# A hybrid attention layer: the v projection fed feature by feature from a transposed copy of x

## The chip, the cores and the metric

One core of a Trainium2 chip. The metric is the device time of one execution in microseconds; lower is better. All data are float32; products are made accurate by splitting each operand into a high part (a reduced-precision float, "fp32r") and a low part (the rest), and by summing three matmul passes: high x high, low x high, high x low.

## The reference

```python
h = rmsnorm(x, pre_g)                      # x: 1024 tokens x 1024 features
p = einsum('btd,de->bte', h, w_in)         # 3328 columns
aq, ak, av, ag, bq, bk, bv, bg = split_projection(p)
ya = sliding_window_sink_attention(aq, ak, av, sinks) * silu(ag)
yb = differential_attention(bq, bk, bv, lam, ...) * silu(bg)
y = einsum('bte,ed->btd', concat(ya, yb), w_out)
return x + rmsnorm(y, post_g)

def rmsnorm(x, g):
    return x * rsqrt(mean(x * x, axis=-1) + 1e-6) * g
```

The norm's factor is one number per token, the gain g one number per feature. v is the 512 columns bv and the 128 columns av.

## The kernel before

The program is written engine by engine, and the engines meet at counting semaphores. It has two stages and an ending.

*The v stage.* v_sb holds tokens on the partitions. The 640 columns are taken as two halves of 320 (`VG`), the 1024 tokens as 8 tiles of 128. One group is one tile and one half: 8 feature slabs x 3 passes = 24 matmuls into one of the two banks of `proj`, then an eviction by ScalarE (`store_v`). Group n is tile n % 8 of half n // 8. To feed it, a tile of x is loaded with tokens on the partitions (`load_x`, three buffers), squared and summed (`square_x`, ScalarE), its factor is made by GpSimd (`root`), it is normalised by VectorE (`norm_x`, L909, against the gain row that TensorE has spread over the partitions into `pre_g`, L1185), turned by eight transposes into `scores` (`turn_x`, L1160), and split into hT_hi (`high_h`, ScalarE, L726) and hT_lo (`low_h`, VectorE, L917). The weights of v are split by ScalarE (`high_wv`), VectorE and GpSimd (both `low_wv`). The tiles go one after another: tile t+1 is turned while tile t is projected.

*The units.* 21 units of 128 columns of w_in (`UNITS`) are projected with the weights stationary and all tokens moving, each in two halves of 512 tokens and six pieces of four matmuls (L1250), into the two banks of `proj`. A schedule written out at build time (`SCHEDULE`) weaves these pieces between the steps of the attention blocks. Unit n needs `w_raw` loaded by SP (`load_w`), w_hi by ScalarE (`high_weights`, L746), w_lo by GpSimd (`low_weights`, L652). SP's queue is in order: the loads for units 0 and 1 are issued during the v stage; ahead of the load for unit 2 stand the two copies of v into `v_shift`, which wait for all 16 evictions:

```python
sp.wait_ge(pads_made, 1)
sp.wait_ge(v_stored, 2 * TILES)
...
for n in range(2, NU):
    load_w(n)
```

VectorE makes the constants of the attention (distances, slopes, lambda: `constants`, L931 to L954) behind its last split of the v stage.

*The ending* projects the output tile by tile (`out_project`, L1354), normalises it and adds x.

Of the kernel before, what the change touches and what calls it, by code (L numbers as in the profile page):

```python
# [75 lines left out]
XS = 3  # L76
WARM_UP = (2, 8)
WV_AT = 5
# [160 lines left out]
def hybrid_layer(nc, x, w_in, w_out, pre_norm_g, post_norm_g, sinks, lambda_q1, lambda_k1,  # L239
# [46 lines left out]
    wv_raw = place("wv_raw", 120, [P, KT, V_WIDTH])  # L286
    x_in = place("x_in", 140, [P, XS, D_MODEL])
    wv_hi = place("wv_hi", 152, [P, KT, V_WIDTH], F32R)
    wv_lo = place("wv_lo", 172, [P, KT, V_WIDTH], F32R)
    g_rows = place("g_rows", 84, [P, D_MODEL])  # L290
    ones = place("ones", 116, [P, P])
    squares = place("squares", 201.75, [P, D_MODEL])
    lam_in = place("lam_in", 118, [P, 4, HEAD_DIM])

# [14 lines left out]
    x_square = column(TILES)  # L309
    x_mean = column(TILES)  # L310
    x_scale = column(TILES)
    min_b = column(2 * B_UNITS)
    sum_b = column(2 * B_UNITS)
    inv_b = column(2 * B_UNITS)
# [11 lines left out]
    neg_half = column(4)  # L326
# [20 lines left out]
    pre_g = banks  # L347
# [3 lines left out]

    x_loaded = [sem(f"x_loaded{i}") for i in range(XS)]
    wv_loaded = [sem(f"wv_loaded{i}") for i in range(6)]
    w_loaded = [sem(f"w_loaded{i}") for i in range(RAW)]
    wo_loaded = [sem(f"wo_loaded{i}") for i in range(WO_RAW)]
    g_row_loaded = sem("g_row_loaded")
    ones_made = sem("ones_made")
    g_zeroed = sem("g_zeroed")
    pre_g_spread = sem("pre_g_spread")
    wv_lo_early = sem("wv_lo_early")  # L360
# [13 lines left out]
    x_squared = sem("x_squared")  # L374
    x_meaned = sem("x_meaned")
    x_scaled = sem("x_scaled")
    x_normed = sem("x_normed")
    x_turned = sem("x_turned")
    h_hi_ready = sem("h_hi_ready")
    h_lo_ready = sem("h_lo_ready")  # L380
    wv_hi_ready = sem("wv_hi_ready")
    wv_lo_ready = sem("wv_lo_ready")
    v_projected = sem("v_projected")
# [44 lines left out]
    def x_turned_at(t):  # L428

        return scores[:, 1024 * (t % 2):1024 * (t % 2) + 1024].rearrange("p (k c) -> p k c", c=P)  # L430

# [25 lines left out]
    def feature_parts(t):  # L457


        return [slice(0, KT // 2), slice(KT // 2, KT)] if t < 2 else [slice(0, KT)]  # L460

    def tile_count(t, part=None):


        before = sum(len(feature_parts(m)) for m in range(t))
        return before + (len(feature_parts(t)) if part is None else part + 1)
# [43 lines left out]
    def wait_proj_free(engine, filling):  # L510

        before = filling - 2
        if before < 0:
            return
        if before < 2 * TILES:
            engine.wait_ge(v_stored, before + 1)
# [42 lines left out]
    v_runs = [[(BV, VG, 0)], [(BV + VG, B_WIDTH - VG, VG), (AV, P, B_WIDTH)]]  # L559

    with nc.Block() as block:

        @block.sync
        def _(sp):
            def load_x(t):
                if t >= XS:
                    sp.wait_ge(x_turned, tile_count(t - XS))
                sp.dma_start(x_in[:, t % XS, :], x[0, t * P:(t + 1) * P, :]).then_inc(x_loaded[t % XS], 16)

            sp.dma_start(g_rows[P - 1:P, :], pre_norm_g[0:1, :]).then_inc(g_row_loaded, 16)  # L570
            for t in range(3):
                if t:
                    load_x(t)
                if t == 2:
                    break
                for part in (2 * t, 2 * t + 1):
                    k = slice(2 * part, 2 * part + 2)
                    sp.dma_start(wv_raw[:, k, 0:VG], w_cols[:, k, BV:BV + VG]).then_inc(wv_loaded[part], 16)
            for i, (first, count, to) in enumerate(v_runs[1]):
                load_x(3 + i)  # L580
                sp.dma_start(wv_raw[:, :, to:to + count],
                             w_cols[:, :, first:first + count]).then_inc(wv_loaded[4 + i], 16)
# [34 lines left out]
            for t in range(5, TILES):  # L617
                load_x(t)
                if t < 7:
                    load_w(t - 5)  # L620
                if t == 5:
                    load_small()
# [24 lines left out]
        def _(pool):  # L647
# [16 lines left out]
            pool.wait_ge(half_made, 1)  # L664
            def low_wv(part):
                k, cols = slice(2 * part, 2 * part + 2), slice(0, VG)
                pool.wait_ge(wv_hi_ready, part + 1)
                nc.gpsimd.tensor_tensor(wv_lo[:, k, cols], wv_raw[:, k, cols], wv_hi[:, k, cols].bitcast(F32),
                                        ALU.subtract).then_inc(wv_lo_early, 1)

            for t in range(TILES):
                pool.wait_ge(x_squared, t + 1)
                nc.gpsimd.tensor_scalar(x_mean[:, t:t + 1], x_square[:, t:t + 1], 1.0, EPS, ALU.mult,
                                        ALU.add).then_inc(x_meaned, 1)
                pool.wait_ge(x_meaned, t + 1)
                root(x_scale[:, t:t + 1], x_mean[:, t:t + 1], 1, x_scaled)
                if t == 0:
                    low_wv(0)
                elif t == 1:
                    low_wv(1)  # L680
                    low_wv(2)
# [3 lines left out]
                           allow_small_or_imprecise_dtypes=True).then_inc(dist_made, 1)  # L685
            for n in (0, 1):
                for part in range(LOWS):
                    low_weights(n, part)
# [29 lines left out]
        def _(act):  # L718
            def high_wv(k, cols, ready):
                act.wait_ge(wv_loaded[ready], 16)  # L720
                nc.scalar.activation(wv_hi[:, k, cols], wv_raw[:, k, cols], ACT.Copy).then_inc(wv_hi_ready, 1)

            def high_h(t, part=0):
                k = feature_parts(t)[part]
                act.wait_ge(x_turned, tile_count(t, part))
                nc.scalar.activation(hT_hi[:, k, t * P:(t + 1) * P], x_turned_at(t)[:, k],  # L726
                                     ACT.Copy).then_inc(h_hi_ready, 1)

            def square_x(t):
                act.wait_ge(x_loaded[t % XS], 16 * (t // XS + 1))  # L730
                if t:
                    act.wait_ge(x_squared, t)
                nc.scalar.activation(squares[:, :], x_in[:, t % XS, :], ACT.Square, scale=D_MODEL ** -0.5,
                                     accum_out=x_square[:, t:t + 1]).then_inc(x_squared, 1)

            def store_v(t, g):
                n = TILES * g + t
                act.wait_ge(v_projected, n + 1)
# [637 lines left out]
```

## Time and profile before

| | us |
|---|---|
| median of 3 runs | 526.04 |
| lowest to highest | 525.56 to 527.71 |
| profiled execution, its own time | 523.85 |
| its span, first to last instruction | 522.0 |
| TensorE busy | 507.3 |
| VectorE busy | 263.9 |
| ScalarE busy | 250.6 |
| GpSimd busy | 115.1 |

The engines are PE (TensorE; PEld are its weight loads), DVE (VectorE), ACT (ScalarE), POOL (GpSimd) and SP. L12 is line 12 of the kernel. A matmul's duration reaches from its start to the end of its pipeline, so durations of neighbours overlap; their pace is the distance of their starts. A plain f32 matmul is two instructions in the profile, one in fp32r a single one.

### The profile page before, as it was taken

What the parts mean: (1) busy time and instruction counts of PE and PEld (TensorE: products, weight loads), DVE (VectorE), ACT (ScalarE), POOL (GpSimd) and SP (SyncE); (2) the same over time, 40 slices, a digit from 0 to 9 for tenths busy, and PEclk for the clock granted to TensorE, in tenths of its full rate; (3) what the DMA queues carried; (4) which work ended last, traced back from release to release, by engine and by line L of the source; (5) the groups of instructions that cost most, each with busy time, mean ns of one, the idle gap of its engine ahead of it and who ended that gap; (6) DMA issues with size and microseconds to landing.
All of it is one profiled execution on the core that took longest, in us unless ns stands there. A gap on an engine that the chain in (4) does not pass through costs nothing.

```text
span 522.0 us, 7538 instructions
## 1 busy us (share of the span) xinstructions
PE 507.3 (97%) x2766; PEld 423.4 (81%) x2766; DVE 263.9 (51%) x648; ACT 250.6 (48%) x615; POOL 115.1 (22%) x157
## 2 busy tenths in 40 slices
PE   7999999999999999999999989999999999999995
PEld 4999997888878787888886767778788888888884
DVE  5655002565565546444547768544654375433332
ACT  5654213556476566556478667533645372322211
POOL 4221204030222120323044243322302260000000
PEclk9999999999999999999999999999999999999998
DMA  8630024130101110110101110111000754332222
GB/s 291 203 123 1 1 46 123 32 80 1 40 15 27 42 41 0 41 40 2 41 1 41 41 42 1 41 41 41 1 1 0 162 162 125 109 130 81 82 84 77
DMA packets 41190, 32.05 MB, mean 61 GB/s; under 512 B 18561, under 2 KB 35905, under 8 KB 41154
## 3 DMA queue, kind: packets, MB, share of 16 engines
q1 hardware_dynamic: 38706, 26.85, 18.4%
q10 hardware_dynamic: 2448, 4.72, 2.4%
q8 instruction: 22, 0.36, 0.3%
q14 instruction: 14, 0.11, 0.1%
HBM read 26.88 MB, written 4.19 MB: 60 GB/s over the span
## 4 chain that ended last, share of the span: by engine, by line
PE 87%; ACT 4%; issue 3%; DVE 3%; DMA 1%; POOL 1%; SPq 0%; DVEq 0%; POOLq 0%; ACTq 0%
PE proj L1250 40%; PE scores L1354 15%; PE proj L1172 11%; PE scores L1269 6%; PE banks L1290 5%; PE banks L1280 3%; PE banks L1335 2%; PE scores L1315 1%; PE banks L1323 1%; PE scores L1160 1%; DMA w_raw<-in_w_in 1%; ACT weights L822 1%; ACT k_stack L802 1%; PE banks L1185 1%; ACT w_hi L746 1%
## 5 line engine op out<-in xcount | busy, mean ns | idle before, releaser
L652 POOL TENSOR_TENSOR w_lo<-w_raw,w_hi 128x256 fp32r<-128x256 f32 x84 | 61.0, 756 | 183.4 <-ACT w_hi L746 183.4
L1250 PE MATMUL proj<-hT_hi,w_hi 128*128 128x512 f32 x336 | 89.9, 400 | 1.1 <-DVE k_stack L1009 0.6
L1250 PE MATMUL proj<-hT_hi,w_lo 128*128 128x512 f32 x336 | 89.4, 400 | 0.0
L1250 PE MATMUL proj<-hT_lo,w_hi 128*128 128x512 f32 x336 | 88.5, 399 | 0.0
L1064 DVE CUSTOM_DVE_ANT_0 weights<-scores,dist_b 128x128 f32<-128x128 f32 (+7 forms) x64 | 45.9, 754 | 53.8 <-PE scores L1269 53.6
L1250 PEld LDWEIGHTS proj<-hT_hi,w_hi 128*128 128x128 f32 x336 | 60.5, 188 | 14.3 <-DVE k_stack L1009 1.0
L1250 PEld LDWEIGHTS proj<-hT_hi,w_lo 128*128 128x128 f32 x336 | 60.6, 188 | 13.3 <-issue 1.9
L1250 PEld LDWEIGHTS proj<-hT_lo,w_hi 128*128 128x128 f32 x336 | 60.6, 188 | 11.8 <-issue 0.8
L822 ACT ACTIVATE weights<-weights,small 128x128 f32<-128x128 f32 (+7 forms) x64 | 49.0, 767 | 15.2 <-DVE small L1064 15.2
L832 ACT ACTIVATE weightsT<-banks 128x512 f32<-128x512 f32 (+3 forms) x48 | 23.6, 491 | 56.0 <-PE banks L1280 55.9
L1269 PE MATMUL scores<-k_stack,q_stack 128*128 128x512 f32 (+3 forms) x192 | 41.8, 353 | 0.0
L1290 PEld LDWEIGHTS banks<-v_sb,weightsT 128*128 128x128 f32 x288 | 36.2, 191 | 4.5 <-ACT weightsT L832 2.1
L1290 PE MATMUL banks<-v_sb,weightsT 128*128 128x128 f32 x288 | 37.8, 276 | 0.1
L656 POOL TENSOR_TENSOR small<-small 128x1 f32<-128x1 f32 (+1 forms) x24 | 17.2, 718 | 85.4 <-DVE small L1137 84.1
L1269 PEld LDWEIGHTS scores<-k_stack,q_stack 128*128 128x128 f32 x192 | 31.9, 189 | 4.9 <-DVE k_stack L1009 0.4
L891 ACT ACTIVATE banks<-scores 128x512 f32<-128x512 f32 x16 | 9.3, 582 | 53.3 <-PE scores L1354 53.3
L1095 DVE CUSTOM_DVE_ANT_0 a_weights<-scores,dist_a,small 128x128 f32<-128x128 f32 x64 | 22.5, 406 | 18.3 <-PE scores L1315 18.3
L1048 DVE SCALAR_TENSOR_TENSOR weights<-weights,small,weights 128x512 f32<-128x512 f32 (+3 forms) x48 | 31.1, 676 | 1.1
L1354 PE MATMUL scores<-wo_hi,hT_hi 128*128 128x512 f32 x128 | 31.6, 389 | 0.0
L1354 PE MATMUL scores<-wo_lo,hT_hi 128*128 128x512 f32 x128 | 31.6, 389 | 0.0
L1354 PE MATMUL scores<-wo_hi,hT_lo 128*128 128x512 f32 x128 | 31.6, 389 | 0.0
L1009 DVE TENSOR_TENSOR k_stack<-proj,k_stack 64x512 fp32r<-64x512 f32 x32 | 22.0, 688 | 12.7 <-ACT k_stack L802 11.9
(114 smaller groups left out, 721.9 us busy)
## 6 DMA issues: line engine op xcount, KB each, us to landing
w_raw<-in_w_in SPq DMA_DIRECT2D x13, 512.0 KB, 3.8
w_raw<-in_w_in SPq DMA_DIRECT2D x16, 256.0 KB, 3.7
x_res<-in_x SPq DMA_DIRECT2D x8, 512.0 KB, 4.5
out<-y_out ACTq DMA_DIRECT2D x16, 256.0 KB, 2.3
x_in<-in_x SPq DMA_DIRECT2D x7, 512.0 KB, 6.0
wv_raw<-in_w_in SPq DMA_DIRECT2D x4, 320.0 KB, 6.0
wo_early<-in_w_out SPq DMA_DIRECT2D x4, 256.0 KB, 4.5
w_raw<-in_w_out SPq DMA_DIRECT2D x4, 256.0 KB, 6.6
```

The lines of the kernel that those rows point to most:

```text
L652: nc.gpsimd.tensor_tensor(w_lo[:, n % SPLIT, k], w_raw[:, n % RAW, k], w_hi[:, n % SPLIT, k].bitcast(F32), ALU.subtract).then_inc(w_lo_rea ...
L822: nc.scalar.activation(w, w, ACT.Exp, scale=-1.0, bias=min_b[:, 2 * u + m:2 * u + m + 1], accum_out=sum_b[:, 2 * u + m:2 * u + m + 1]).the ...
L832: nc.scalar.activation(weightsT[:, 4 * r:4 * r + blocks, :], turned[:, 0:P * blocks].rearrange("p (b q) -> p b q", q=P), ACT.Copy).then_in ...
L1009: nc.vector.tensor_tensor(k_lo[part, m, tokens], source[own, :], k_hi[own, m, tokens].bitcast(F32), ALU.subtract).then_inc(stack_lo, 1)
L1048: nc.vector.scalar_tensor_tensor(w0, w1, mix_b[:, u:u + 1], w0, ALU.mult, ALU.add).then_inc(b_mixed, 1)
L1064: nc.vector.tensor_tensor_reduce(out=weights_1[:, 0:keys] if m else weights_0[:, u % 2, 0:keys], in0=scores[:, 1024 * m:1024 * m + keys], ...
L1095: nc.vector.tensor_tensor_reduce(out=a_weights_of(c)[:, j, :], in0=scores[:, a_scores_at(c, j):a_scores_at(c, j) + P], in1=dist_a[:, min(c ...
L1172: done = nc.tensor.matmul(proj[:, n % 2, 0:VG], h[:, k, tokens], w[:, k, cols], start=(first and k == ks[0]), stop=(last and k == ks[-1]))
L1250: last = nc.tensor.matmul(to, w[:, slot, k, :], h[:, k, HALF * half:HALF * half + HALF], start=(p == 0 and k == first), stop=(p == PIECES ...
L1269: last = nc.tensor.matmul(scores[:, 1024 * m + first:1024 * m + first + width], q_stack[head][m][:, P * block_:P * block_ + P], k[:, m, fi ...
L1290: last = nc.tensor.matmul(mixed[:, P * (u % 4):P * (u % 4) + P], weightsT[:, b, :], v_sb[:, b, P * head:P * head + P], start=(b == 0), sto ...
L1354: last = nc.tensor.matmul(scores[:, at:at + HALF], y[:, k, tokens], w[:, k, cols], start=(p == 0 and k == 0), stop=(p == PASSES - 1 and k ...
```

## The change

The host hands over x a second time, transposed (`xT`, features first), and the gain as a column per slab (`g_columns`). The kernel no longer turns x.

- Slabs of 128 features are loaded: x_all[:, k, :] (all 1024 tokens) and the 320 columns of w_in for the first half of v, in turn, k = 0 to 7. All are issued on SP's queue with no wait; slab 0 of x comes in two halves from ScalarE's queue.
- v's operand is x times the gain, without the token's factor. hT_hi and hT_lo hold this first (`high_x`, `low_x`). The factor is applied per token (that is, per partition) at the eviction: `store_v` has a scale.
- Seven token tiles are summed side by side, one PSUM bank each, slab by slab (`K_MAJOR = 7`). The eighth tile and the whole second half of v follow group by group (24 matmuls each).
- The squares are summed over slabs elementwise (ScalarE squares, VectorE adds), then over the partitions by eight one-column matmuls (`x_sums`). GpSimd takes all 8 x 128 roots in one instruction.
- The normalised h is still needed for the units. The factors are put on diagonals, spread over all partitions by two f32 matmuls (`scale_rows`), x_all is normalised in place beside the second half of v, and hT_hi and hT_lo are written a second time (`high_again` and h_lo_again) tile by tile, each after the group that reads the old tile.
- The iotas of GpSimd move to its start; the constants move ahead of the normalisation on VectorE. The splits of the second half's weights are four pieces on ScalarE and GpSimd.

```diff
-            for t in range(TILES):
-                store_v(t, 0)
-                if t + 3 < TILES:
-                    square_x(t + 3)
-                if t + 2 < TILES:
-                    high_h(t + 2)
...
+            def high_x(k):
+                for part, tokens in enumerate(token_parts(k)):
+                    act.wait_ge(x_loaded[k + part if k == 0 else k + 1], 16)
+                    nc.scalar.activation(hT_hi[:, k, tokens], x_all[:, k, tokens], ACT.Copy,
+                                         scale=g_column[:, k:k + 1]).then_inc(h_hi_ready, 1)
+            def square_x(k):
+                if k >= 3:
+                    act.wait_ge(squares_added, k - 2)
+                to = squared[k % 2] if k else square_sum
+                nc.scalar.activation(to[:, :], x_all[:, k, :], ACT.Square).then_inc(x_squared, 1)
...
+                nc.scalar.activation(v_sb[:, t, VG * g:VG * (g + 1)], v_bank(n), ACT.Copy,
+                                     scale=x_scale[:, t:t + 1]).then_inc(v_stored, 1)
+            def high_again(t):
+                tokens = slice(P * t, P * t + P)
+                act.wait_ge(x_normed, KT)
+                act.wait_ge(v_projected, TILES + t + 1)
+                nc.scalar.activation(hT_hi[:, :, tokens], x_all[:, :, tokens], ACT.Copy).then_inc(h_hi_again, 1)
...
+            for k in range(KT):
+                high_x(k)
+                if k:
+                    act.wait_ge(wv_loaded[k], 16)
+                    nc.scalar.activation(wv_hi[:, 0, k], wv_raw[:, 0, k], ACT.Copy).then_inc(wv_hi_ready, 1)
+                square_x(k)
...
+            for k in range(1, KT):
+                low_x(k)
+                low_wv(k)
+                if k > 1:
+                    add_squares(k - 1)
+            add_squares(KT - 1)
+            dve.wait_ge(x_summed, 1)
+            nc.vector.tensor_scalar(x_mean, x_sums, 1.0 / D_MODEL, EPS, ALU.mult, ALU.add).then_inc(x_meaned, 1)
...
+            constants()
+            dve.wait_ge(scale_spread, 2)
+            for k in range(KT):
+                nc.vector.scalar_tensor_tensor(x_all[:, k, :], x_all[:, k, :], g_column[:, k:k + 1],
+                                               scale_rows[:, :], ALU.mult, ALU.mult).then_inc(x_normed, 1)
...
+            for _ in range(WARM_UP):
+                nc.tensor.matmul(turned[:, 0:P], ones[:, :], ones[:, :], start=True, stop=True)
+            for k in range(KT):
...
+                if k < KT - 1:
+                    for p, ready in enumerate((h_hi_ready, h_lo_ready)):
+                        for part, tokens in enumerate(token_parts(k)):
+                            pe.wait_ge(ready, part_count(k, part))
+                            for t in range(tokens.start // P, min(tokens.stop // P, K_MAJOR)):
+                                project_v(t, k, p)
+                    pe.wait_ge(wv_lo_ready, k + 1)
+                    for t in range(K_MAJOR):
+                        project_v(t, k, 2)
...
+            pe.wait_ge(squares_added, KT - 1)
             for t in range(TILES):
+                done = nc.tensor.matmul(x_sums[:, t:t + 1], square_sum[:, P * t:P * t + P], ones[:, 0:1],
+                                        start=True, stop=True)
+            done.then_inc(x_summed, 1)
+            for n in range(K_MAJOR, 2 * TILES):
+                if n >= TILES:
+                    wait_v_bank(pe, n)
+                if n == TILES + 1:
+                    pe.wait_ge(diagonals_made, TILES)
+                    pe.wait_ge(v_stored, TILES)
+                    for half in range(2):
+                        cols = slice(HALF * half, HALF * half + HALF)
+                        nc.tensor.matmul(scale_rows[:, cols], ones[:, :], diagonals[:, cols],
+                                         start=True, stop=True).then_inc(scale_spread, 1)
...
+                        if n == 0:
+                            pe.wait_ge(h_hi_again, TILES // 2 * (half + 1))
                     which, first = divmod(p * KP, KT)
+                    if n == 0 and which == 1:
+                        pe.wait_ge(h_lo_again, TILES // 2 * (half + 1))
```

`token_parts(k)` is two halves of 512 tokens for k = 0 and 1, all 1024 tokens for the others.

## Rows read from the trace of the kernel before

**Rows 1.** The page: busy time of the engines, and the span in 40 slices.

```profile
PE 507.3 (97%) x2766; PEld 423.4 (81%) x2766; DVE 263.9 (51%) x648; ACT 250.6 (48%) x615; POOL 115.1 (22%) x157
...
PEclk9999999999999999999999999999999999999998
```

**Rows 2.** The chain of waits: start, length, what, count.

```profile
38.48 0.87 PE scores L1160 x8
39.35 34.03 PE proj L1172 x232
73.94 0.73 SPq L627
75.43 5.59 DMA w_raw<-in_w_in
81.05 1.06 ACT w_hi L746
...
84.77 11.18 PE proj L1250 x48
...
154.59 1.87 PE banks L1290 x16
```

**Rows 3.** Timeline of TensorE, end of the v stage (wait in brackets).

```profile
72.04 1.34 PE L1172 MATMUL proj<-wv_lo,hT_hi 128*128 128x320 f32 x8
73.21 2.00 PE L1250 MATMUL proj<-hT_hi,w_hi 128*128 128x512 f32 x8
...
84.77 2.11 PE L1250 MATMUL proj<-hT_hi,w_hi 128*128 128x512 f32 x8 [0.49 <-DVE q_stack L1004]
```

**Rows 4.** Timeline of TensorE, the start.

```profile
1.69 0.69 PE L1179 MATMUL proj<-ident 128*128 128x128 f32 x2 [1.69 <-POOL ident L662]
3.19 3.75 PE L1185 MATMUL banks<-g_rows,ones 128*128 128x512 f32 x4 [0.81 <-DVE g_rows L965]
6.74 1.20 PE L1188 MATMUL proj<-ident 128*128 128x128 f32 x8
...
9.06 0.56 PE L1172 MATMUL proj<-wv_hi,hT_hi 128*128 128x320 f32 x2 [0.25 <-ACT hT_hi L726]
```

**Rows 5.** Windows of 1 us: busy by engine, granted clock, DMA share, GB/s.

```profile
1.00:2.00 1.00, 0.31 (x2) 0.29 (x2) 0.91 (x1) 0.86 (x1) 0.39 (x2) 1.00 0.36 82
2.00:3.00 1.00, 0.38 (x2) 0.00 (x0) 0.82 (x1) 0.42 (x1) 0.00 (x0) 1.00 0.91 348
3.00:4.00 1.00, 0.81 (x1) 0.50 (x2) 0.09 (x1) 0.02 (x1) 0.00 (x0) 1.00 0.92 299
4.00:5.00 1.00, 1.00 (x2) 0.34 (x1) 0.00 (x0) 1.00 (x2) 0.00 (x0) 1.00 0.91 288
```

**Rows 6.** Groups of instructions by shape, 0 to 75 us: busy, mean ns of one.

```profile
L909 DVE SCALAR_TENSOR_TENSOR x_in<-x_in,small,banks 128x1024 f32<-128x1024 f32 x6 | 7.7, 1282 | 9.3 <-POOL small L656 9.3
L733 ACT ACTIVATE squares<-x_in 128x1024 f32<-128x1024 f32 x7 | 7.4, 1055 | 1.9 <-DMA x_in<-in_x 1.9
...
L917 DVE TENSOR_TENSOR hT_lo<-scores,hT_hi 128x1024 fp32r<-128x1024 f32 x6 | 7.3, 1219 | 2.7 <-ACT hT_hi L726 2.7
L739 ACT ACTIVATE v_sb<-proj 128x320 f32<-128x320 f32 x16 | 7.0, 438 | 31.7 <-PE proj L1172 31.5
L726 ACT ACTIVATE hT_hi<-scores 128x1024 fp32r<-128x1024 f32 x6 | 6.2, 1029 | 4.5 <-PE scores L1160 4.4
...
L668 POOL TENSOR_TENSOR wv_lo<-wv_raw,wv_hi 128x640 fp32r<-128x640 f32 x3 | 4.6, 1557 | 0.0
L656 POOL TENSOR_TENSOR small<-small 128x1 f32<-128x1 f32 x8 | 4.4, 553 | 0.7
...
L721 ACT ACTIVATE wv_hi<-wv_raw 128x640 fp32r<-128x640 f32 x4 | 2.8, 732 | 0.0
...
L726 ACT ACTIVATE hT_hi<-scores 128x512 fp32r<-128x512 f32 x4 | 2.3, 595 | 3.7 <-PE scores L1160 3.7
...
L922 DVE TENSOR_TENSOR wv_lo<-wv_raw,wv_hi 128x640 fp32r<-128x640 f32 x1 | 0.8, 817 | 0.0
```

**Rows 7.** Timeline of VectorE, first and last of the constants.

```profile
44.63 0.22 DVE L931 CUSTOM_DVE_ANT_0 junk<-lam_in 128x64 f32<-128x64 f32 x1
...
48.64 0.11 DVE L954 MEMSET dist_a<- 128x64 f32 x1
```

More of the change, by code:

```diff
@@ L284, in hybrid_layer @@
     small = place("small", 206.25, [P, 392])
[L286 to L292, printed above, removed]
+    x_all = place("x_all", 120, [P, KT, SEQ])
+    wv_hi = place("wv_hi", 152, [P, 2, KT, VG], F32R)
+    wv_lo = place("wv_lo", 172, [P, 2, KT, VG], F32R)
+    wv_raw = place("wv_raw", 72, [P, 2, KT, VG])
+    squared = [place("squared0", 92, [P, SEQ]), place("squared1", 192, [P, SEQ])]
+    diagonals = place("diagonals", 92, [P, SEQ])
+    square_sum = place("square_sum", 201.75, [P, SEQ])
     lam_in = place("lam_in", 118, [P, 4, HEAD_DIM])
+    ones = place("ones", 119.5, [P, P])
     wo_hi = place("wo_hi", 96, [P, KT, D_MODEL], F32R)
@@ L615, in load_wo @@
                     to += count
[L617 to L622, printed above, removed]
+            load_w(0)
+            load_small()
+            load_w(1)
             sp.wait_ge(pads_made, 1)
@@ L685, in _ @@
                            allow_small_or_imprecise_dtypes=True).then_inc(dist_made, 1)
+            pool.wait_ge(half_made, 1)
+            for part in range(KT // 2):
+                if part == 2:
+                    pool.wait_ge(x_meaned, 1)
+                    root(x_scale, x_mean, TILES, x_scaled)
+                k = slice(2 * part, 2 * part + 2)
+                pool.wait_ge(wv_hi_late, part + 1)
+                nc.gpsimd.tensor_tensor(wv_lo[:, 1, k], wv_raw[:, 1, k], wv_hi[:, 1, k].bitcast(F32),
+                                        ALU.subtract).then_inc(wv_lo_late, 1)
             for n in (0, 1):
@@ L718, in _ @@
         def _(act):
[L719 to L727, printed above, removed]
@@ L962, in make_lambda @@
                 nc.vector.tensor_scalar(neg_lam, lam_dif, LAMBDA_INIT, None, ALU.subtract).then_inc(consts_made, 1)
-            for part in (slice(0, 96), slice(96, P - 1)):
-                nc.vector.memset(g_rows[part, :], 0.0).then_inc(g_zeroed, 1)
-            norm_x(0)
-            dve.wait_ge(x_loaded[1], 16)
-            dve.wait_ge(x_squared, 1)
-            nc.vector.tensor_tensor_reduce(out=squares[:, :], in0=x_in[:, 1, :], in1=x_in[:, 1, :],
-                                           scale=1.0 / D_MODEL, scalar=0.0, op0=ALU.mult, op1=ALU.add,
-                                           accum_out=x_square[:, 1:2]).then_inc(x_squared, 1)
@@ L1164, in _, with project_v @@
             V_PASSES = ((hT_hi, wv_hi), (hT_lo, wv_hi), (hT_hi, wv_lo))
-            def project_v(t, g, p, ks, first=False, last=False):
-                n = TILES * g + t
+            def project_v(n, k, p):
+                g, t = divmod(n, TILES)
                 h, w = V_PASSES[p]
-                tokens, cols = slice(P * t, P * t + P), slice(VG * g, VG * (g + 1))
-                for k in ks:
-                    done = nc.tensor.matmul(proj[:, n % 2, 0:VG], h[:, k, tokens], w[:, k, cols],
-                                            start=(first and k == ks[0]), stop=(last and k == ks[-1]))
-                if last:
-                    done.then_inc(v_projected, 1)
@@ L1177, in _ @@
-            pe.wait_ge(ident_made, 2)
-            for _ in range(WARM_UP[0]):
-                nc.tensor.transpose(proj[:, 1, 0:P], ident[:, :], ident[:, :])
-            pe.wait_ge(ones_made, 1)
-            pe.wait_ge(g_zeroed, 2)
-            pe.wait_ge(g_row_loaded, 16)
-            for half in range(2):
-                cols = slice(HALF * half, HALF * half + HALF)
-                nc.tensor.matmul(pre_g[:, cols], ones[:, :], g_rows[:, cols],
-                                 start=True, stop=True).then_inc(pre_g_spread, 1)
@@ L1228, in _ @@
-            pe.wait_ge(wv_hi_ready, 6)
-            for t in range(TILES):
-                wait_proj_free(pe, TILES + t)
-                project_v(t, 1, 0, ALL, first=True)
-                project_v(t, 1, 1, ALL)
-                if t == 0:
-                    pe.wait_ge(wv_lo_ready, 3)
-                project_v(t, 1, 2, ALL, last=True)
+                return nc.tensor.matmul(v_bank(n), h[:, k, P * t:P * t + P], w[:, g, k, :],
+                                        start=(k == 0 and p == 0), stop=(k == KT - 1 and p == PASSES - 1))
```

300 lines of the change are left out of this document (129 added, 171 removed).

## The prediction

> **What bounds the kernel now.** I read the page first: TensorE is busy 97% of the span at a granted clock of 9 tenths in every slice but the last, so time is won by taking work off TensorE or by closing an idle stretch of it [rows 1]. Then the chain of waits: from the fourth transposed tile on it is TensorE alone, eight transposes in 0.87 us and 24 matmuls of the v projection between them, until 232 matmuls in a row end in 34.03 us, 0.1467 us each [rows 2]. So one group of 24 matmuls (one token tile, one half of v) costs 3.52 us, and the 16 groups 56.3 us. The 64 transposes (8 tiles of 0.87 us) cost 6.96 us more. The first matmul of the projection units starts at 73.21 us [rows 3]. 73.21 - 56.3 - 6.96 leaves 9.9 us: that is what the start costs, in pauses and in slow instructions.
>
> The timeline of TensorE shows what is in these 9.9 us [rows 4]. It waits for the identity until 1.69, spreads the gain row from 3.19 (held by the zeroing of 127 rows on VectorE), runs eight idle transposes, and has its first v matmul at 9.06. The four instructions of the spread run from 3.19 to 6.74, 0.89 us each; they are f32 with 512 columns. f32 instructions with 128 columns take 1.87 us for 16, 0.117 each, in the middle of the kernel [rows 2], so 512 columns should take four times that, 0.47. They took about twice as long: though the granted clock of those microseconds reads 1.00, the high level of 2.4 GHz [rows 5], these instructions ran as at the lower one, 1.2 GHz. TensorE had done nothing but two transposes before.
>
> **What goes.** (a) The 64 transposes: -6.96 us. (b) The chain ahead of the first matmul, x to square to root to normalise to transpose to h_hi, ends at 9.06. Of the 9.9 us, 9.06 less the 0.87 of the first tile's transposes lie ahead of that matmul, and 1.7 us are pauses behind it (h_hi and h_lo of the first two tiles); both go. The squares, the normalisation and the splits that leave VectorE and ScalarE were beside TensorE later than that and give nothing by themselves.
>
> **What comes at the start.** Features first, the first matmul needs the gain column, the first half slab of x, and slab 0 of the weights. By the windows of DMA, 82 + 348 + 299 = 729 KB had moved by 4.0 us and 1,017 KB by 5.0 [rows 5]. Slab 0 is 512 KB of x plus 160 KB of weights, 688 thousand bytes; half of x is there at about 3.3 and the weights slab at about 3.6. ScalarE splits the half (0.60 us for 512 columns [rows 6]) until about 4.0, VectorE copies the weights meanwhile. The warm-up is now eight f32 matmuls of 128 columns, 16 instructions. At the lower clock one takes twice 0.107 to 0.117; from about 1.1 us they last until about 4.7. So v starts near 4.7 us (bounds: 4.2 if the clock rises early, 6.0 if slab 0 is there only with the 1,017 KB of 5.0 us and a split follows). If TensorE's instructions keep the low pace until 6.74 as in [rows 4], slab 0 loses up to 1.1 us; I take 0.4, as it is now continuously busy from 1.1 and not from 3.19.
>
> **The slab stage, who paces it.** Per slab TensorE has 7 tiles x 3 passes = 21 matmuls x 0.1467 = 3.08 us. VectorE: h_lo of 1024 columns with a scale 1.28 us (the scalar-tensor-tensor row), wv_lo of 320 columns about 0.49 (a line through 0.82 at 640 and 1.22 at 1024), the sum of squares 1.22: 2.99 us. ScalarE: h_hi 1.03, wv_hi about 0.46 (0.73 at 640, less 320 columns at the 0.84 ns that lie between 0.60 at 512 and 1.03 at 1024), square 1.05: 2.5 us [rows 6]. DMA: 688 KB at 288 to 348 GB/s is 2.0 to 2.4 us [rows 5]. TensorE is the slowest by 0.09 over VectorE, and busy times overlap a little with the next start, so it paces the stage. But ScalarE's square k waits for the addition of k-2, so ScalarE and VectorE are locked together; walking the two orders by hand, h_lo of slab 3 is ready at 13.8 and of slab 7 at 25.8, wv_lo of slab 7 at 26.3, where TensorE comes at 4.7 + 7 x 3.08 = 26.3. I allow 0.4 us of small waits (bounds 0 and 2.0, the latter if VectorE's period is 3.3). Eight slabs: 8 x 3.08 = 24.6.
>
> **What is added on TensorE.** x_sums: 8 f32 matmuls of one column, 16 instructions. Each loads 128 weight columns; the nearest row is 0.117 us per f32 instruction, 1.9 us in all, with one column in place of 128. I take 1.4 (bounds 0.9 and 3.4, at half speed). The sums of squares are ready at about 28.7, before the slabs end at 29.7-30: no wait. scale_rows: two f32 matmuls of 512 columns, 4 instructions at 0.47: 1.9 us at the full rate; 3.6 if they went as in [rows 4]. I take 1.8.
>
> **Covers of the rest.** After the sums come group 7 (3.52 us), then group 8, which needs one v bank emptied. The chain in between is mean on VectorE, root on GpSimd (0.55 us), one eviction (0.44): about 1.6 us with hand-overs, cover 3.52. GpSimd must first do two of the late wv_lo parts (1.56 us each [rows 6]), from about 26.8 to 29.9, before the mean is there; parts 3 and 4 end near 35, needed near 36.8. Group 9 needs only the eight diagonals (ready near 34); the constants, 44.63 to 48.75 before, 4.1 us [rows 7], go from about 34 to 38 while group 8 runs, and the spread ends near 39.7. If this cover were gone, h would be late by what is missing, not v. The normalisation is 8 x 1.28 = 10.3 us on VectorE, to about 50; ScalarE then makes h_hi again for tile m once group 8+m has been read, in the order of the evictions: tiles 0-3 by about 58, tile 7 at 64.9 + 0.25 + 0.44 + 1.03 = 66.6, and h_lo of it at 67.9. Unit 0, first half, wants tiles 0-3 at about 65 (cover 7 us); its second half wants tile 7 at 65 + 5.6 = 70.6 (24 matmuls, 0.233 each by the 48 of the chain [rows 2]; cover 3.9). So the second pass of splits costs nothing.
>
> On the SP queue everything of v is issued with no wait, then w_raw 0, the six small loads, w_raw 1; 6.8 MB for v at 300 GB/s are in by 23 us, the small ones by 30. The load for unit 2 still stands behind the wait for all 16 evictions: issue 73.94, landed 81.05, and its split [rows 2]. That chain is tied to the end of v and not to the clock on the wall, so it moves with it; TensorE's 0.49 us pause at 84.77 stays [rows 3]. Behind it the schedule is unchanged.
>
> **Sum.** 4.7 + 0.4 (clock) + 24.6 + 0.4 (waits) + 1.4 + 7.04 (groups 7, 8) + 1.8 + 24.64 (groups 9 to 15) = 65.0 us, against 73.21: -8.2 us. The profiled execution has 522.0 of span and 523.85 of its own time, the runs a median of 526.04; the difference of 2.2 us is outside what I change, so I take the 8.2 off the median: 517.8.
>
> **Rivals.**
> - *Forecast, TensorE paces the slabs* (0.75): 515.5 to 520.
> - *The suppliers pace them* (0.12). For it: VectorE's 2.99 is only 3% under 3.08, and the lock with ScalarE adds hand-overs. Against: TensorE's own share of work is the only one that can't shrink. At 3.3 to 3.6 us a slab it costs 8 x 0.2 to 0.5 = 1.8 to 4.2 us: 519.5 to 522.
> - *The clock falls in the slab loop* (0.04), the one on the other side. The loop over features spends 3.08 us of TensorE's work per load of data; with pauses between slabs TensorE may run as in [rows 4]. A stretch at half speed costs half its length; the gain of 8.2 is eaten after 16.4 us of it, 5 of the 8 slabs; all 8 slabs give 24.6 more, 542. Against it: the old kernel also had 1.7 us of pauses behind 9.06, and its granted clock stayed at the high level [rows 1]. The Trainium skill ("TensorE: Matmul & The Clock Gate", section on HAM oscillation) describes just this loop, one feature tile per load with a wait of some microseconds, as the one that falls to the low clock at every tile. By that rule the time would be up to 542; by the supply worked out above the waits are tenths of a microsecond, and it would not apply.
> - *h is late at unit 0* (0.04): the second pass of splits stands behind evictions and the normalisation. Each microsecond beyond the 3.9 of cover costs one; 8 us late gives 522.
> - *Nothing comes through* (0.02): the 8 us reappear before a load; 526. Against: no wait of SP is later than its evictions.
> - *Better* (0.03): start at 4.2, cheap sums, no waits: 515.0.
>
> **Range and chances.** The bounds add up to -1.8 and, in the usual mix, +3.5 around 517.8, with half a microsecond between medians: 515.2 to 521.3. A measurement tells 0.5%, 2.6 us, from nothing. Faster by that (under 523.4): the forecast, the better case, the suppliers, most of late h: 0.92. Same 0.04 (nothing comes through, part of the clock case and of late h). Slower 0.04.
>
> **What would show it.** The first matmul of unit 0 at 65 us (64 to 68). The first v matmul near 4.7. In the slab stage, a wait of TensorE on h_hi or h_lo over 0.3 us per slab would show the suppliers as the pace; spacing of 320-column matmuls over 0.15 with no wait, the clock. x_sums 1.4 and scale_rows 1.8 us. No wait of TensorE at the first two halves of unit 0. From there on the timeline equal to the old one, shifted by one number. I am wrong if VectorE's additions of squares hold ScalarE's h_hi, if group 8 waits for the root, or if the constants wait for the small loads and push the normalisation.

## The result and the profile after

The changed kernel took 521.42 us (median of 4, 520.26 to 522.22) where the old one took 525.8 (median of 4): ratio of new to old 0.990, 95% interval 0.9881 to 0.9919. Forecast were 517.8 us, 8.2 less than before, and a range up to 521.3. The direction held; 4.4 us came through, about half, and the time lies 0.1 us above the range. The same kernel in two later sets of runs gave 518.9 us (ratio 0.987, 0.9848 to 0.989) and 520.79 us (0.9897, 0.9875 to 0.992). So single medians of it spread over 2.5 us, and part of the question is what spreads them.

The page of the profiled execution (its own time 522.18): span, busy times, clock in 40 slices.

```profile
span 520.4 us, 7482 instructions
...
PE 504.6 (97%) x2724; PEld 422.9 (81%) x2724; DVE 286.2 (55%) x672; ACT 259.8 (50%) x622; POOL 116.1 (22%) x143
...
PEclk9999999999999999999999999999999989999999
```

Against [rows 1], TensorE has 2.7 us less of busy time, VectorE 22 and ScalarE 9 us more, and one slice near 420 us has a lower clock. The timeline of TensorE through the v stage, where [rows 3, 4] were read before:

```profile
0.97 3.78 PE L1170 MATMUL banks<-ones 128*128 128x128 f32 x16 [0.97 <-POOL ones L668]
5.65 1.41 PE L1165 MATMUL scores<-wv_hi,hT_hi 128*128 128x320 f32 x4 [0.90 <-ACT hT_hi L723]
...
7.66 1.27 PE L1165 MATMUL scores<-wv_hi,hT_lo 128*128 128x320 f32 x4
...
9.53 0.84 PE L1165 MATMUL scores<-wv_lo,hT_hi 128*128 128x320 f32 x4
...
10.64 0.75 PE L1165 MATMUL scores<-wv_hi,hT_hi 128*128 128x320 f32 x4
...
13.72 0.75 PE L1165 MATMUL scores<-wv_hi,hT_hi 128*128 128x320 f32 x4
...
32.20 1.84 PE L1195 MATMUL banks<-ones,square_sum 128*128 128x1 f32 x16
33.91 1.41 PE L1165 MATMUL banks<-wv_hi,hT_hi 128*128 128x320 f32 x8
...
41.02 1.88 PE L1206 MATMUL banks<-diagonals,ones 128*128 128x512 f32 x4
...
67.38 2.00 PE L1234 MATMUL proj<-hT_hi,w_hi 128*128 128x512 f32 x8
...
79.02 2.12 PE L1234 MATMUL proj<-hT_hi,w_hi 128*128 128x512 f32 x8 [0.57 <-DVE q_stack L1010]
```

Slab 1 starts at 10.64, slab 2 at 13.72: 3.08 us, as computed, and no wait stands in brackets anywhere from 10.64 to 67.38. Slab 0 takes 4.99 us, from 5.65 to 10.64. Its groups of four 320-column matmuls last 1.41 and 1.27 us where later ones last 0.75. Up to about 9.5 the matmuls start 0.27 to 0.30 us apart, later 0.147: half the pace, as at 1.2 GHz, though the granted clock of these microseconds reads 1.00. The units begin at 67.38 against 73.21 [rows 3]: 5.8 us earlier. At the end of the kernel only 1.6 us of span are left of it. The rest is lost between the last unit and the output projection. The timeline of TensorE there, then the window of 426 to 428 us (its length, busy time of PE, PEld, DVE, ACT and POOL, granted clock, DMA share, GB/s):

```profile
421.75 1.98 PE L1234 MATMUL proj<-hT_hi,w_lo 128*128 128x512 f32 x8
425.82 3.52 PE L1340 MATMUL scores<-wo_hi,hT_hi 128*128 128x512 f32 x8 [2.10 <-ACT hT_hi L882]
429.14 2.20 PE L1340 MATMUL scores<-wo_hi,hT_lo 128*128 128x512 f32 x8
```
```profile
426.00:428.00 2.00, 2.00 (x6) 1.59 (x7) 1.88 (x5) 2.00 (x5) 0.00 (x0) 0.53 0.00 0
```

TensorE waits 2.1 us for the first high part of y (the gated output of both attentions, which the output projection multiplies by w_out) and then does eight matmuls in 3.3 us that take 1.8 otherwise; the granted clock of these 2 us is 0.53, nearly all of it the low level (1.2 GHz). In the old kernel's profiled execution its last unit ended and the output projection began with no pause:

```profile
427.39 1.98 PE L1250 MATMUL proj<-hT_hi,w_lo 128*128 128x512 f32 x8
429.20 1.99 PE L1354 MATMUL scores<-wo_hi,hT_hi 128*128 128x512 f32 x8
```

w_out is loaded and split in eight slabs, 0 to 7; their high parts (wo_hi) come from ScalarE, the low parts (wo_lo) of even slabs from GpSimd, of odd ones from VectorE. The timelines of VectorE and of GpSimd in the changed kernel show what y waited for:

```profile
409.96 2.86 DVE L1038 TENSOR_TENSOR wo_lo<-wo_early,wo_hi 128x1024 fp32r<-128x1024 f32 x1 [0.48 <-ACT wo_hi L785]
...
415.56 1.21 DVE L1038 TENSOR_TENSOR wo_lo<-w_raw,wo_hi 128x1024 fp32r<-128x1024 f32 x1
419.34 2.29 DVE L1038 TENSOR_TENSOR wo_lo<-wo_early,wo_hi 128x1024 fp32r<-128x1024 f32 x1 [2.57 <-ACT wo_hi L785]
421.56 0.67 DVE L1027 SCALAR_TENSOR_TENSOR gate<-gate,proj 128x512 f32<-128x512 f32 x1
422.26 2.17 DVE L1034 TENSOR_TENSOR out_B<-gate,out_B 128x512 f32<-128x512 f32 x1
```
```profile
409.06 2.68 POOL L696 TENSOR_TENSOR wo_lo<-wo_early,wo_hi 128x1024 fp32r<-128x1024 f32 x1 [8.80 <-ACT wo_hi L785]
412.20 2.88 POOL L696 TENSOR_TENSOR wo_lo<-w_raw,wo_hi 128x1024 fp32r<-128x1024 f32 x1 [0.46 <-ACT wo_hi L785]
418.14 2.41 POOL L696 TENSOR_TENSOR wo_lo<-wo_early,wo_hi 128x1024 fp32r<-128x1024 f32 x1 [3.05 <-ACT wo_hi L785]
420.92 2.96 POOL L696 TENSOR_TENSOR wo_lo<-w_raw,wo_hi 128x1024 fp32r<-128x1024 f32 x1 [0.37 <-ACT wo_hi L785]
```

The gate of the last unit stands in VectorE's queue behind wo_lo of w_out slab 5. That waits for ScalarE's split, which waits for the slab's load, which SP issued only when wo_lo of slab 1 was done at 412.8. The load took 5.3 us, here as in after_third; in after_repeat, where the pause is shorter, it took 4.3.

The second cause is that a VectorE operation with both inputs in SBUF and a GpSimd subtraction do not run at the same time: whichever starts second seems to stand still until the other is done. That is read from these rows: the subtraction of 1.21 us that starts at 409.96 ends 1.08 us behind GpSimd's (411.74), the one of 419.34 ends 1.08 us behind GpSimd's (420.55), and the product out_B, 0.69 us alone, begins at 422.26 and ends at 424.43, 0.55 us behind GpSimd's (423.88). So y also waited for GpSimd's share of slab 6. The gate at 421.56, one of whose inputs (proj) lies in PSUM, took 0.67 us beside GpSimd, no more than elsewhere. In the old kernel's trace the same product began at 426.49, ahead of GpSimd's subtraction of slab 6 (426.86), and took 0.69.

### The profile page after: what moved, and what is told of

It reads as the page before. It is cut to its first block, busy times and chain, and to the rows that moved or that the text cites. A ratio compares the mean times of both kernels' runs of the same rounds, so it can differ in the third digit from the quotient of the medians.

```text
span 520.4 us, 7482 instructions
## 1 busy us (share of the span) xinstructions
PE 504.6 (97%) x2724; PEld 422.9 (81%) x2724; DVE 286.2 (55%) x672; ACT 259.8 (50%) x622; POOL 116.1 (22%) x143
## 4 chain that ended last, share of the span: by engine, by line
PE 83%; ACT 5%; issue 4%; DVE 3%; DMA 3%; POOL 1%; SPq 0%; DVEq 0%; POOLq 0%; ACTq 0%
PE proj L1234 37%; PE scores L1340 15%; PE scores L1165 8%; PE scores L1255 6%; PE banks L1276 5%; PE banks L1266 3%; PE banks L1321 2%; PE proj L1165 1%; PE banks L1165 1%; PE scores L1301 1%; PE banks L1309 1%; DMA w_raw<-in_w_in 1%; DMA wo_early<-in_w_out 1%; ACT weights L823 1%; ACT k_stack L803 1%
## 5 line engine op out<-in xcount | busy, mean ns | idle before, releaser
L662 POOL TENSOR_TENSOR w_lo<-w_raw,w_hi 128x256 fp32r<-128x256 f32 x84 | 63.0, 778 | 173.3 <-ACT w_hi L748 173.3
L1340 PE MATMUL scores<-wo_hi,hT_hi 128*128 128x512 f32 x128 | 33.2, 403 | 2.1 <-ACT hT_hi L882 2.1
L666 POOL TENSOR_TENSOR small<-small 128x4 f32<-128x4 f32 (+2 forms) x17 | 14.4, 846 | 91.9 <-DVE small L1143 88.1
L1340 PEld LDWEIGHTS scores<-wo_hi,hT_hi 128*128 128x128 f32 x128 | 24.8, 195 | 7.7 <-ACT hT_hi L882 2.5
```

The source lines that it names most:

```text
L662: nc.gpsimd.tensor_tensor(w_lo[:, n % SPLIT, k], w_raw[:, n % RAW, k], w_hi[:, n % SPLIT, k].bitcast(F32), ALU.subtract).then_inc(w_lo_rea ...
L1340: last = nc.tensor.matmul(scores[:, at:at + HALF], y[:, k, tokens], w[:, k, cols], start=(p == 0 and k == 0), stop=(p == PASSES - 1 and k ...
```

## Experiments

**The kernel again, twice, unaltered.**

> The changed kernel once more, unaltered, to see how its runs spread. Theory 1 (the pause of TensorE between the last unit and the output projection, 2.1 us with 1.5 us of half-speed matmuls behind it, comes and goes from run to run, as it hangs on when two loads of w_out land): two groups of times, near 520.4 and 522.2 us, the lower with a mean granted clock of 0.999 and the upper with 0.995. Rival (the pause is in every run and the spread is something else): one clock value in all runs.

> The changed kernel unaltered, a third set of runs and a third trace. If the first set (521.4 us, full pace only from 9.4 us) was one end of a spread that each execution draws anew, this one lies between 518.5 and 521.5 us, with the full pace from some time between 5.6 and 9.4 us and the pause ahead of the output projection between 1 and 2.3 us. If the chip decides, its times stay within 0.5 us of one of the two sets.

Measured: 518.9 us (518.42 to 520.56) and 520.79 us (518.58 to 522.04), on two chips. The two traces, at the start of TensorE; first after_repeat:

```profile
5.74 0.82 PE L1165 MATMUL scores<-wv_hi,hT_hi 128*128 128x320 f32 x4 [1.09 <-ACT hT_hi L723]
...
8.90 0.79 PE L1165 MATMUL scores<-wv_hi,hT_hi 128*128 128x320 f32 x4
...
65.67 2.00 PE L1234 MATMUL proj<-hT_hi,w_hi 128*128 128x512 f32 x8
```

and after_third:

```profile
5.71 1.40 PE L1165 MATMUL scores<-wv_hi,hT_hi 128*128 128x320 f32 x4 [0.96 <-ACT hT_hi L723]
...
10.83 0.75 PE L1165 MATMUL scores<-wv_hi,hT_hi 128*128 128x320 f32 x4
...
67.56 2.00 PE L1234 MATMUL proj<-hT_hi,w_hi 128*128 128x512 f32 x8
```

The first v matmul is at 5.7 in all three. Slab 0 takes 3.16 us where TensorE was at its full pace and 4.99 or 5.12 where it was not yet. From slab 1 to the units it is 56.77, 56.74 and 56.73 us. So nearly all that differs up to the units is when the pace rises, up to 1.9 us. The pause ahead of the output projection was in all three, but not of one size: 1.2 us, with no half-speed stretch behind it, in after_repeat (span 516.6); 1.8 and 2.1 with one in the others (520.2, 520.4). "Comes and goes" was wrong for these three traces, "varies" holds, and the mean granted clock of a run does not tell the two apart (0.996 in after_repeat, whose pause kept the high level). The chip is not the cause by itself: the third set alone reaches from 518.6 to 522.0, and its median lies 0.6 us or more from both earlier ones.

**The table load ahead of the waits.**

```diff
+            act.wait_ge(ones_made, 1)
+            nc.scalar.activation(primed[:, :], ones[:, 0:1], ACT.Copy).then_inc(act_primed, 1)
             act.wait_ge(g_loaded, 16)
```

> The changed kernel with a one-column activation ahead of ScalarE's waits, so that the table load (1.28 us, now from 3.49) is done before the first data. Theory 1: first h_hi from about 3.6 us, first v matmul near 4.8 in place of 5.65, TensorE without the 0.9 us pause behind its warm-up, and so the full pace sooner: 0.9 us from the start and up to 1.9 us from slab 0, 1 to 2.8 us faster than the changed kernel in the stage up to the units. Rival (the clock rises at its own time, whatever the pause): only 0.9 us earlier start, of which half is lost at the low pace: 0.4 us. Rival 2 (weights and x are the bound at the start): the first matmul stays at 5.6, as the copy of the weights starts at 4.91.

Measured: 520.26 us (518.63 to 520.68), ratio 0.9879 (0.986 to 0.9897); the unaltered kernel beside it had 0.9869 (0.9848 to 0.989). No gain can be told. In the trace the first v matmul came at 5.08, 0.6 us earlier, and it now waited for the weights (timeline of TensorE):

```profile
5.08 1.11 PE L1169 MATMUL scores<-wv_hi,hT_hi 128*128 128x320 f32 x4 [0.32 <-DVE wv_hi L970]
...
65.63 2.00 PE L1238 MATMUL proj<-hT_hi,w_hi 128*128 128x512 f32 x8
```

Rival 2 was right in part: of the 0.95 us hoped for 0.57 came, then TensorE had to wait for the first weights, which landed at 4.69 here (4.9 to 5.5 in the traces of the changed kernel and of late_order). And the units began at 65.63, with after_repeat's 65.67, as the first matmuls were slower: slab 0 took 3.72 us against 3.16 there.

**The last gate ahead of the split of w_out slab 5**, in the new kernel and in the old one.

```diff
-        if outs and at % OUT_EVERY == 0:
+        if outs and at % OUT_EVERY == 0 and at != last + 4:
             steps.append(("split_out", outs.pop(0)))
```

> The changed kernel with the split of w_out slab 5 (and with it 6 and 7) placed behind the last unit's first gate, so that the gate on VectorE and the first y split on ScalarE do not stand behind the landing of slab 5. Theory 1: no pause of TensorE ahead of the output projection in any run, no half-speed stretch there; all runs like the fast group, 520.4 us, so a median 0.5 to 1.5 us lower. Rival (the pause only moves to the wait for slabs 6 and 7 inside the first output tile): same times, with PE waiting on wo_hi or wo_lo.

> The old kernel with the same reordering as late_order (split of w_out slab 5 and after behind the last unit's first gate). Theory 1 (the pause ahead of the output projection is in most runs of the old kernel too, the profiled one of 523.85 us being one without it): 1 to 2 us faster than the old kernel, near 525. Rival (the pause comes from the change, by an altered timing of loads): the same as the old kernel, 526.5.

Measured: 517.45 us (516.99 to 518.29), ratio 0.9833 (0.9816 to 0.9849), beside the changed kernel's 518.9; and for the old kernel 523.73 us (523.51 to 524.85) against 526.35, ratio 0.9955 (0.9941 to 0.9969). All four runs of late_order are faster than all fourteen of the changed kernel (518.42 at the least). In late_order TensorE goes over without a pause (timelines of VectorE and of TensorE):

```profile
417.84 0.69 DVE L1027 SCALAR_TENSOR_TENSOR gate<-gate,proj 128x512 f32<-128x512 f32 x1 [2.18 <-ACT gate L816]
418.56 0.82 DVE L1034 TENSOR_TENSOR out_B<-gate,out_B 128x512 f32<-128x512 f32 x1
419.31 1.21 DVE L1038 TENSOR_TENSOR wo_lo<-wo_early,wo_hi 128x1024 fp32r<-128x1024 f32 x1
```
```profile
420.64 1.98 PE L1234 MATMUL proj<-hT_hi,w_lo 128*128 128x512 f32 x8
422.45 1.98 PE L1340 MATMUL scores<-wo_hi,hT_hi 128*128 128x512 f32 x8
```

TensorE waits for no wo_hi or wo_lo either, so the pause did not move elsewhere. Both kernels gained, the new one 1.5 us, the upper end of what was expected, the old one 2.6, more than was expected. So the pause most likely belongs to the old kernel too, in most of its runs. No trace of the unaltered old kernel shows it, but the next experiment's, an old kernel with less to do, has one of 1.3 us; and the old kernel's profiled execution of 523.85, without a pause, was one of its fastest and equals what it does with the reordering (span 522.0 against 521.9). Compared profile with profile, the change therefore looks worse (1.6 us) than it is. With the pause taken out of both kernels it is worth 523.73 - 517.45 = 6.3 us by the medians, 6.6 by the two spans (521.9, 515.3).

**Fewer transposes in the old kernel.**

```diff
                     for k in range(ks.start, ks.stop):
+                        if t >= 2 and k < ks.stop - 1:
+                            continue
```

> The old kernel with only the last of the eight transposes of token tiles 2 to 7 (the other slabs hold what tiles 0 and 1 left, so v and h are wrong there): 42 transposes of 64 fewer. Theory 1 (TensorE's time in this stage is a plain sum): 42 x 0.109 = 4.6 us earlier at the first unit and as much at the end, 521.3. Rival (the stage waits for h_hi and h_lo instead, or the end gives it back): the first unit less than 3 us earlier, or the end less than 3 us though the first unit is 4.6 earlier.

Measured: 524.52 us (521.9 to 525.3) against 526.51, ratio 0.9963 (0.9945 to 0.9981): 2.0 us. The rival was right. The first unit starts at 71.85, 1.4 us earlier. Of the 4.6 us, 0.4 went in a later start and 2.8 in pauses of TensorE behind it. 2.1 us of pauses are listed as waits, where the old kernel's list has 0.5 (waits by line, columns: total, times, longest):

```profile
PE proj L1174 <- DVE hT_lo L917: 1.4, 2, 0.7
...
PE proj L1174 <- ACT hT_hi L726: 0.7, 3, 0.2
```

The transposes of the next tile filled time in which a tile was being split. Most of what they cost could be had only together with the chain of norm, turn and split, which the change removed: in its slab stage TensorE waits for nothing.

**One more pass of VectorE per slab.**

```diff
                 low_wv(k)
+                if k > 1:
+                    dve.wait_ge(extra_done, k - 1)
+                nc.vector.tensor_tensor(v_sb[:, 0:2, 0:HALF], x_all[:, k, :].rearrange("p (a b) -> p a b", b=HALF),
+                                        hT_hi[:, k, :].bitcast(F32).rearrange("p (a b) -> p a b", b=HALF),
+                                        ALU.subtract).then_inc(extra_done, 1)
```

> The changed kernel with one more VectorE subtraction of 128x1024 per slab for slabs 1 to 7 (1.2 us each, its result unused and overwritten). VectorE's period in the slab stage was 2.73 us against TensorE's 3.08. Theory (TensorE paces it with 0.35 us of room per slab): the period becomes 2.73 + 1.14 = 3.87 us, TensorE waits for h_lo, and the stage ends 7 x 0.79 = 5 to 5.5 us later, time 523.5 to 524.5. Rival (ScalarE's or DMA's pace counts and VectorE's does not): no more than 2 us.

Measured: 525.29 us (524.84 to 529.4), 6.4 above the changed kernel's 518.9 and 3.9 above its slowest median. VectorE's rows in the slab stage have the computed period, 14.61 to 18.48, 3.87 us, and TensorE waits for them (timelines of VectorE and of TensorE):

```profile
14.61 1.28 DVE L908 SCALAR_TENSOR_TENSOR hT_lo<-x_all,small,hT_hi 128x1024 fp32r<-128x1024 f32 x1
...
18.48 1.28 DVE L908 SCALAR_TENSOR_TENSOR hT_lo<-x_all,small,hT_hi 128x1024 fp32r<-128x1024 f32 x1
```
```profile
23.68 0.85 PE L1171 MATMUL scores<-wv_hi,hT_lo 128*128 128x320 f32 x4 [0.52 <-DVE hT_lo L908]
...
31.92 0.41 PE L1171 MATMUL scores<-wv_hi,hT_hi 128*128 128x320 f32 x1 [2.05 <-DVE wv_lo L917]
```

The units begin at 71.88, 6.2 us behind after_repeat's. The forecast held in size, but not all of it is waiting: the listed waits of the stage behind its start add up to 3.5 us, and behind the last, of 2.05 us, the granted clock fell to 0.50 and 13 matmuls took 3.4 us, 1.5 more than at the full pace. So the room that VectorE has, 3.08 - 2.73 = 0.35 us per slab, is real: one pass of 1.2 us per slab all but ate the whole gain (7.6 us in the earlier set).

**All second splits behind the last eviction.**

```diff
-HIGH_AGAIN = [[], [], [], [0, 1], [2, 3], [4], [5, 6], [7]]
+HIGH_AGAIN = [[], [], [], [], [], [], [], [0, 1, 2, 3, 4, 5, 6, 7]]
```

> The changed kernel with all eight second splits of h_hi behind the last eviction of v instead of between the evictions. Theory (they are hidden only by the place they have; four tiles are due at the first unit): unit 0 waits for four splits, 4 x 1.0 us and hand-overs, 4.5 us, its second half for the last of eight and h_lo by another 0 to 1 us; the load chain of unit 2 is covered by the same shift: time 4 to 6 us above the changed kernel, 523 to 525. Rival (the pauses are swallowed by the chain v_stored to w_raw to w_hi to q_stack, which held TensorE at unit 1 anyway): under 2 us.

Measured: 525.57 us (523.95 to 527.53), 6.7 above the changed kernel's 518.9 and 4.2 above its slowest median. The wait is as computed, but it has a second price (timeline of TensorE):

```profile
70.35 3.75 PE L1234 MATMUL proj<-hT_hi,w_hi 128*128 128x512 f32 x8 [4.49 <-ACT hT_hi L742]
73.90 2.92 PE L1234 MATMUL proj<-hT_lo,w_hi 128*128 128x512 f32 x8
76.66 1.98 PE L1234 MATMUL proj<-hT_hi,w_lo 128*128 128x512 f32 x8
```

Behind 4.49 us of idling 16 matmuls take 6.3 us, 3.6 otherwise: 2.7 us more for the lower clock, granted at 0.50 from 70 to 74 us. The rival got only its 0.5 us: the wait at unit 1 is gone (4.49 + 2.68 - 0.54 = 6.6).

**One warm-up matmul in place of eight.**

```diff
-WARM_UP = 8
+WARM_UP = 1
```

> The changed kernel with one warm-up matmul instead of eight, so that TensorE does nothing from 1.4 us to its first v matmul. Theory (what TensorE did before decides when it reaches the full pace; with eight it was there between 5.6 and 9.4 us in the executions seen): the full pace comes 3 to 4 us later, near 9 us or after, slabs 0 and 1 lose 1.5 to 2 us: 520.5 to 521 against 518.9. Rival (the pace rises at a time that has nothing to do with the warm-up): the same time as the changed kernel within 0.5 us.

Measured: 519.39 us (518.31 to 522.62), ratio 0.9879 (0.9849 to 0.9908), against the unaltered kernel's 520.79 in the same set. The forecast loss is not there; nor does the 1.4 us the other way count, as the intervals overlap. With runs that spread over 4.3 us the rival, no difference, is not shown either. In its trace slab 0 took 5.4 us (5.95 to 11.32), with the full pace from 10.8: later than in any trace with eight, but little worse than the 4.99 and 5.12 there.

**The parts together**: late order, table first, the first weights issued ahead of the gain column, ten warm-up matmuls.

> The changed kernel with late_order, table_first, the weights of slab 0 issued ahead of the gain column, and a warm-up of ten matmuls. If the parts add: first v matmul at 4.6 to 4.9 us, no pause at the end, 516.5 to 517.5 us, 0.5 to 1 us below late_order (517.45). Rival (the first slab runs at the low pace when TensorE comes to it sooner, so the earlier start is half lost): the same as late_order within 0.5 us.

Measured: 516.55 us (516.45 to 517.03), ratio 0.9816 (0.9802 to 0.983) against late_order's 0.9833 (0.9816 to 0.9849). It has the lowest median here. The intervals of the two overlap, so that the start adds something is likely and not shown; that the reordering beats the changed kernel is shown. The first v matmul came at 5.57, not at 4.6 to 4.9. The ten warm-up matmuls were in its way until then, and without them it could have come little sooner: the gain column, now issued behind the weights, landed only at 4.71, and half a slab of h_hi takes 0.7 us (timelines of TensorE and of ScalarE):

```profile
0.97 4.63 PE L1175 MATMUL banks<-ones 128*128 128x128 f32 x20 [0.97 <-POOL ones L671]
5.57 1.34 PE L1170 MATMUL scores<-wv_hi,hT_hi 128*128 128x320 f32 x4
```
```profile
4.71 1.34 ACT L726 ACTIVATE hT_hi<-x_all,small 128x512 fp32r<-128x512 f32 x2 [1.57 <-DMA small<-in_g_columns]
```

## Why the prediction came out as it did

The units began at 67.38 where the sum had 65.0: 0.95 us too late a start, 1.5 too little for the clock in slab 0, 0.3 too little for x_sums, less the 0.4 of waits that did not come. Each term by itself:

- *First v matmul at 4.7*: 5.65. The half slab of x landed nearly as computed, 3.49 against 3.3, but ScalarE's table load came behind it instead of ahead of it (timelines of ScalarE and of VectorE):

```profile
3.49 1.28 ACT L723 ACT_TABLE_LOAD   x1 [3.49 <-DMA x_all<-in_xT]
4.79 1.34 ACT L723 ACTIVATE hT_hi<-x_all,small 128x512 fp32r<-128x512 f32 x2
```
```profile
4.91 0.33 DVE L966 CAST wv_hi<-wv_raw 128x320 fp32r<-128x320 f32 x1 [4.91 <-DMA wv_raw<-in_w_in]
```

  In the old kernel the table load began at 1.14, in the shadow of the first load. The weights of slab 0 landed at 4.91, not at 3.6: 556 KB had moved by 4.0 us, not the 729 of the old kernel. By the x chain the loss is 0.95 us, and table_first shows that 0.6 of it is all that can be had before the weights bind. The Trainium skill ("ScalarE: Activation LUTs", What ACT_TABLE_LOAD costs) gives about 1283 ns for the load, which the trace has too; where the load ends up in the queue is what counted here.
- *0.4 us for the clock in slab 0*: 1.9 in this execution, 0.1 in after_repeat, 2.0 in after_third. This is the largest mis-sized term before the units. The bound of 1.1 rested on one execution of the old kernel, in which the pace rose near 7 us. It was taken for a property of the kernel, and it varies between executions of one program.
- *Slabs 24.6 with waits 0.4*: from slab 1 on 3.08 us each and no wait. VectorE's period was 2.73, not 2.99: each busy time overlaps the next start by about 0.1 us, and summing them overstates the period (timeline of VectorE):

```profile
13.42 1.28 DVE L907 SCALAR_TENSOR_TENSOR hT_lo<-x_all,small,hT_hi 128x1024 fp32r<-128x1024 f32 x1
...
16.15 1.28 DVE L907 SCALAR_TENSOR_TENSOR hT_lo<-x_all,small,hT_hi 128x1024 fp32r<-128x1024 f32 x1
```

  ScalarE did wait for the additions, up to 0.28 us per slab, and it cost TensorE nothing.
- *x_sums 1.4, groups 7 and 8 7.04, spread 1.8, groups 9 to 15 24.64*: 1.71, 7.11 and, from 41.02 to 67.38, 26.36: 24.64 for seven groups leaves 1.72 for the spread. Slab 1 to units was forecast as 21.6 + 34.9 = 56.5 and is 56.7.
- *The second splits cost nothing, cover 3.9 to 7 us*: right, no wait at unit 0; tile 7's h_hi was done at 69.05, 3.8 us before its use at 72.85. What lies ahead of them was not as computed: the root took 1.66 us in place of 0.55, the eight diagonals were ready at 40.3 and not near 34 (0.7 us before TensorE's spread), and the normalisation began at 44.3, not 39.7. The cover took it. again_last shows the price if the cover goes, 4.5 us and 2.7 for the clock.
- *The chain v_stored to w_raw moves with the stage, 0.49 us at unit 1*: right, 0.57.
- *Behind it the timeline is the old one, shifted by one number*: it held for 356 us and failed at the far end (units from 67.4 to 423.6, 356.2 us; before 73.2 to 429.2, 356.0). Then 4.0 of the 5.6 us that were there at the last unit's end went in the hand-over to the output projection. The prediction had one execution of the old kernel to go by, in which the first high part of y was done at 428.5, 0.7 us before TensorE came for it; it did not price this place and booked the 2.2 us between that execution and the median as "outside what I change". They were most likely this pause, as before_late_order's 2.6 us suggest. That the gain was taken off the median and not off this execution is luck: the pause (1.2 to 2.1 us in the changed kernel's traces, with or without the half-speed stretch) seems to be in both medians and so falls out of their difference. What is left of the 8.2 us then depends, at least in part, on when the full pace comes at the start: 4.4 us in the first set, 7.6 and 5.3 in the two later ones.
- *Rivals*: the suppliers did not pace the slabs, and the clock did not fall in the slab loop (the granted clock reads 1.00 up to 420 us, and the pace is the full one from 10.64). The Trainium skill ("TensorE: Matmul & The Clock Gate", HAM oscillation) speaks of a wait for data between the feature tiles; here was none, so this trace neither bears it out nor speaks against it. extra_pass has a wait ahead of its last slab, for VectorE and not for a load, 2.05 us long, and the low pace behind it. Being late at unit 0 and nothing at all did not happen either.

What stays open: when TensorE reaches its full pace after the start. Across the traces of the changed kernel and its variants it lies between about 5.7 and 10.8 us. The latest is the one with a single warm-up matmul, but 9.5 to 10 came with eight too, so no run tied it to the warm-up. And why the first set of runs was 2.5 us above the second: the start (1.7) and the hand-over (0.9 more of pause and 1.1 more of slow matmuls) account for 3.7 of the 3.8 us between the two traces' spans, but that is not shown for every run. Nor was GpSimd's subtraction of slab 6 moved by itself, so its share of the pause is read from the trace and not tested.

## What to carry to other kernels

When a change shifts a whole stage, check the next tight hand-over behind it for how much room it has, and from more than one execution: here one trace of the old kernel had 0.7 us of room where each trace of the changed one had a pause of 1.2 to 2.1 us, and reordering the splits of w_out gave 1.5 us on the new kernel and 2.6 on the old. Reckon an engine's period from start to start, not by adding busy times. Taking out a transpose that fills another engine's latency does not give back its duration; that comes only when the chain it was covering goes too.

## What was not expected of the hardware

- VectorE work with two inputs in SBUF and a subtraction of GpSimd took turns. On VectorE 1.21 us became 1.5 to 2.9 and 0.69 became 1.4 to 2.7, and the end lay 1.1 us (1024 columns) or 0.55 us (512) behind GpSimd's end in the traces of the old kernel, the changed one, after_repeat and no_warm_up. It goes the other way too: the subtraction of GpSimd that begins at 412.20 in the changed kernel, while VectorE's runs until 412.82, took 2.88 us, and one that VectorE joined later (418.14) took 2.41. The Trainium skill ("VectorE: DVE Perf Modes", Two Vector instructions with no wait between them) mentions in passing a second SBUF read interface shared with GpSimd; these rows agree with it.
- The pace of TensorE at the start differed between executions of the same program by 1.9 us, while the row of the granted clock read 1.00 for all of them.
- Pauses of TensorE of 1.8, 2.05, 2.1 and 4.5 us (after_third, extra_pass, the changed kernel, again_last) were followed by the low clock; those of 1.2 to 1.6 us ahead of the output projection (after_repeat, few_turns, table_first, extra_pass, again_last, no_warm_up) were not. No run varied the length of a pause alone.
